# Two-layer decoder trunk: the sums of the third and fourth conditioning vectors of layer 0 shared out anew between VectorE, ScalarE and GpSimd

## What is computed

```python
c_act = silu(c)                                   # c: (1, 1024)
for l in range(2):
    mod = c_act @ w_ada[l] + b_ada[l]             # six vectors of 1024
    sh1, sc1, gt1, sh2, sc2, gt2 = split(mod, 6)
    h = x * (1 + sc1) + sh1
    y = hybrid_mixer(h, ...)                      # window attention + top-k attention picked by index scores
    x = layer_norm(alpha * x + (1 + gt1) * y, ...)
    h = x * (1 + sc2) + sh2
    y = swiglu(h, ...)
    x = layer_norm(alpha * x + (1 + gt2) * y, ...)
```

## Time and profile before

| | us |
|---|---|
| median of 3 runs (1275.62 to 1276.37) | 1276.03 |
| the profiled execution | 1276.25 |
| its span in the trace | 1274.6 |
| TensorE busy in it | 1235.8 (97%) |
| VectorE busy | 801.5 (63%) |
| ScalarE busy | 510.5 (40%) |
| GpSimd busy | 274.2 (22%) |

### The profile page before, as it was taken

One profiled execution on the slowest core, in us unless ns is written; L12 is line 12 of the kernel. 1 busy time (PEld: TensorE's weight loads), 2 busy tenths in 40 slices (PEclk: granted clock), 3 DMA queues, 4 the chain that ended last, 5 costly groups with the idle time before them and its releaser, 6 DMA issues. The chain is left out here.

```text
span 1274.6 us, 18347 instructions
## 1 busy us (share of the span) xinstructions
PE 1235.8 (97%) x6394; PEld 1031.6 (81%) x6394; DVE 801.5 (63%) x1400; ACT 510.5 (40%) x1027; POOL 274.2 (22%) x281
## 2 busy tenths in 40 slices
PE   6999989999999999999999999999999999999997
PEld 5778876889888888888888688778988888888886
DVE  6889997677777764333676699856733355433338
ACT  3555568345232212222145466862643321222220
POOL 4027236600111010000007367570000000000000
PEclk9999999999999999999999999999999999999999
DMA  9672012334878554222523120112232223332211
GB/s 358 240 270 79 33 51 67 132 116 150 279 264 270 193 168 175 90 93 98 171 94 117 66 67 2 37 63 84 75 124 99 97 101 132 99 98 89 94 65 66
DMA packets 44850, 158.30 MB, mean 124 GB/s; under 512 B 5872, under 2 KB 5872, under 8 KB 44784
## 3 DMA queue, kind: packets, MB, share of 16 engines
q1 hardware_dynamic: 30528, 109.07, 24.8%
q0 software_dynamic: 12960, 47.19, 10.9%
q10 hardware_dynamic: 1296, 1.17, 0.3%
HBM read 155.31 MB, written 2.10 MB: 123 GB/s over the span
## 5 line engine op out<-in xcount | busy, mean ns | idle before, releaser
L631 PE MATMUL bank<-hT_hi,w_hi 128*128 128x512 f32 x640 | 249.5, 390 | 0.0
L633 PE MATMUL bank<-hT_hi,w_lo 128*128 128x512 f32 x640 | 249.0, 389 | 0.0
L632 PE MATMUL bank<-hT_lo,w_hi 128*128 128x512 f32 x640 | 249.0, 389 | 0.0
L1967 DVE TENSOR_TENSOR w_lo<-w_raw,w_hi 128x1024 fp32r<-128x1024 f32 x88 | 107.9, 1226 | 147.0 <-ACT w_hi L1434 147.0
L1280 ACT ACTIVATE w_hi<-w_raw 128x1024 fp32r<-128x1024 f32 x96 | 100.7, 1062 | 202.8 <-PE bank L633 189.0
L1434 ACT ACTIVATE w_hi<-w_raw 128x1024 fp32r<-128x1024 f32 x88 | 93.0, 1057 | 161.1 <-PE bank L633 155.8
L631 PE MATMUL bank<-w_hi,hT_hi 128*128 128x512 f32 (+2 forms) x392 | 148.1, 378 | 2.9 <-ACT pq L1316 2.0
L1544 DVE TENSOR_TENSOR w_lo<-w_raw,w_hi 128x1024 fp32r<-128x1024 f32 x88 | 114.1, 1310 | 53.6 <-ACT w_hi L1280 52.2
L633 PE MATMUL bank<-w_hi,hT_lo 128*128 128x512 f32 (+2 forms) x392 | 142.6, 364 | 0.0
L632 PE MATMUL bank<-w_lo,hT_hi 128*128 128x512 f32 (+2 forms) x392 | 142.3, 363 | 0.0
L633 PEld LDWEIGHTS bank<-hT_hi,w_lo 128*128 128x128 f32 x640 | 120.1, 188 | 25.3
(11 more groups left out here) (207 smaller groups left out, 2199.5 us busy)
## 6 DMA issues: line engine op xcount, KB each, us to landing
w_raw<-in_weights SPq DMA_DIRECT2D x184, 512.0 KB, 3.5
ada_w<-in_w_ada POOLq DMA_DIRECT2D x80, 512.0 KB, 5.2
ada_w<-in_w_ada SPq DMA_DIRECT2D x4, 512.0 KB, 6.6
qT<-in_w_ada SPq DMA_DIRECT2D x4, 512.0 KB, 10.0
xs<-in_x SPq DMA_DIRECT2D x4, 512.0 KB, 15.4
g_row<-in_ln_row POOLq DMA_DIRECT2D x4, 512.0 KB, 5.2
b_row<-in_ln_row POOLq DMA_DIRECT2D x4, 512.0 KB, 6.1
trunk_out<-xs SPq DMA_DIRECT2D x8, 256.0 KB, 2.1
```

The lines of the kernel that those rows point to most:

```text
L631: pe.matmul(dst, a_hi, b_hi, start=first, stop=False)
L632: pe.matmul(dst, a_hi, b_lo, start=False, stop=False)
L633: return pe.matmul(dst, a_lo, b_hi, start=False, stop=last)
L1967: nc.vector.tensor_tensor(w_lo[:, s, :], w_raw[:, s, :], w_hi[:, s, :].bitcast(F32), ALU.subtract).then_inc(lo_ready, 1)
```

## The change

The last four pieces of group 2 (`ASIDE`, n = 20 to 23) leave VectorE. ScalarE scales each with one activation (`scale_aside`) into a buffer of its own: `g_row`, `b_row` and two halves of `pq[:, 1]`, which are free at that time; two of them stand before the evacuation of chunk 1, two behind it. GpSimd adds the four up with three additions of 128x1024 in `g_row`, between its issues of loads, and `reduce_mod(2)` sums both `ada_acc` and `g_row` on TensorE, with 16 products instead of 8. The slots of pieces 20 to 23 are loaded again when ScalarE has scaled them (`aside_scaled`), and counts of `ada_used` leave them out (`ada_count`). VectorE now sums all eight pieces of group 3 before the index scores: two before the `rope` calls on the index keys, six after `convert` of weight pieces 10 and 11. The four pieces amid the attention are gone, and GpSimd issues the loads up to piece 35 before its `rope` of the queries. `evacuate(0, 2, t)` waits for the three additions, and GpSimd's `ln_rows(1)` for `reduce_mod(2)`.

```diff
...
 QB_AT = (9, 21, 30, 45)
 
 
-ASIDE_AT = (12, 18, 24, 30)
-ASIDE_FROM = 3 * KD + 4
+ASIDE = range(2 * KD + 4, 3 * KD)
 
 WO_AT = (42, 47, 52, 57)
 GATE_AT = 63
...
             pT = sb("pT", [P, PT_RING, 512], on=att)
 
         prob = pq[:, 1]
+
+        aside = [g_row[:], b_row[:]]
+        aside += [pq[:, 1, 2 * n:2 * n + 2, :].rearrange("p a s -> p (a s)") for n in range(2)]
 
         y = pk[:].rearrange("p t n -> p (t n)").rearrange("p (b n) -> p b n", b=2)
 
...
 
             b, at = (2 + k // 4, (k % 4) * P) if g == 0 else (6, k * 64)
             return bank[b][:, at:at + n]
+
+        def ada_count(n):
+
+            return n if n <= ASIDE[0] else n - len(ASIDE)
 
         def columns_to(g):
 
...
             def ada_fetch(upto):
                 while fetched[0] < upto:
                     n = fetched[0]
-                    pool.wait_ge(ada_used, n - RING + 1)
+                    if n - RING in ASIDE:
+                        pool.wait_ge(aside_scaled, n - RING - ASIDE[0] + 1)
+                    else:
+                        pool.wait_ge(ada_used, ada_count(n - RING + 1))
                     if n < 2 * KD + RING:
 
                         pool.wait_ge(mod_reduced, 2)
...
                     ada_fetch(2 * KD + 4 + RING)
                     pool.wait_ge(tables_ready, 1)
                 if l == 0:
-                    ada_fetch(3 * KD + 4)
+                    ada_fetch(3 * KD + 2)
+                    for i in range(1, 4):
+                        pool.wait_ge(aside_scaled, i + 1)
+                        if i > 1:
+                            pool.wait_ge(aside_summed, i - 1)
+                        nc.gpsimd.tensor_tensor(aside[0], aside[0], aside[i], ALU.add).then_inc(aside_summed, 1)
+                        ada_fetch(3 * KD + (2, 4, 4)[i - 1])
+                    pool.wait_ge(aside_summed, 3)
                 else:
                     for t in range(T):
                         rope(l, 0, t)
...
                 if l == 0:
                     pool.wait_ge(small_in, 16 * 4)
                 if l == 0:
-                    ada_fetch(ASIDE_FROM + RING)
+                    ada_fetch(4 * KD + RING)
                 for t in range(T):
                     rope(l, 2, t)
                 for t in range(T):
                     rope_keys(l, t)
                 for i in range(64 + LAG_ROOT):
-                    if i in ASIDE_AT and l == 0:
-                        ada_fetch(ASIDE_FROM + RING + ASIDE_AT.index(i) + 1)
                     if i in ROPE_AT:
                         rope(l, 4, ROPE_AT.index(i))
                     if i == ROPE_AT[-1]:
...
                         gained_low_half(l, WO_AT.index(i))
                 if l == 0:
                     ada_fetch(5 * KD + RING)
+                    pool.wait_ge(mod_reduced, 3)
                 ln_rows(2 * l + 1)
                 for t in range(T):
                     rsqrt(l, 8 + t)
...
 
             def reduce_mod(g, b):
 
-                pe.wait_ge(ada_used, (g + 1) * KD)
+                pe.wait_ge(ada_used, ada_count((g + 1) * KD))
+                if g == 2:
+                    pe.wait_ge(aside_summed, 3)
                 for k in range(KD):
                     m = pe.matmul(bank[b][:, k:k + 1], ada_acc[:, g % 2, k * P:(k + 1) * P], ones[:, 0:1],
-                                  start=True, stop=True)
+                                  start=True, stop=g != 2)
+                    if g == 2:
+                        m = pe.matmul(bank[b][:, k:k + 1], aside[0][:, k * P:(k + 1) * P], ones[:, 0:1],
+                                      start=False, stop=True)
                 m.then_inc(mod_reduced, 1)
 
             def first_mod(g, vector, first):
...
                 src = bank[QB_BANK if c == 4 else BANKS[c] + t]
                 if c in (0, 2, 4):
 
+                    if l == 0 and c == 2:
+                        act.wait_ge(aside_summed, 3)
                     if l > 0 and c == 0:
                         act.wait_ge(qk_transposed, at_chunk(l - 1, 4, t))
                     elif l > 0 and c == 2:
...
                     nc.scalar.activation(v_a[:, t, 0:P], src[:, P:2 * P], ACT.Copy)
                     nc.scalar.activation(v_a[:, t, P:P + HD], src[:, P:P + HD], ACT.Copy).then_inc(proj_evac, 1)
 
+            def scale_aside(i):
+
+                n = ASIDE[i]
+                act.wait_ge(ada_in[n % RING], 16 * ((n - 2 * KD) // RING + 1))
+                if i < 2:
+                    act.wait_ge(mod_reduced, 2)
+                else:
+                    act.wait_ge(tables_ready, 1)
+                nc.scalar.activation(aside[i], ada_w[:, n % RING, :], ACT.Copy, scale=cc[:, 1, n % KD:n % KD + 1])\
+                    .then_inc(aside_scaled, 1)
+
             def copy_q(l, c, t):
                 act.wait_ge(qk_transposed, at_chunk(l, c, t))
                 if c == 4 and t == 0:
...
                 for c in range(2):
                     if c == 1:
                         convert(l, C0P[2] + 2)
+                    if c == 1 and l == 0:
+                        scale_aside(0)
+                        scale_aside(1)
                     for t in range(T):
                         if (l, c) != (0, 0):
                             evacuate(l, c, t)
                         if c == 0 and t == 1:
                             convert(l, C0P[1] + 2)
+                    if c == 1 and l == 0:
+                        scale_aside(2)
+                        scale_aside(3)
                     convert(l, C0P[c + 1] + 3 + c)
                 for t in range(T):
                     copy_q(l, 0, t)
...
                         residual(l, WO0, WO0_ORDER[0], True)
                         if l == 0:
                             ada_group(4, 4, 7)
-                    if i in ASIDE_AT and l == 0:
-                        n = ASIDE_FROM + ASIDE_AT.index(i)
-                        ada_group(n // KD, n % KD, n % KD + 1)
                 conv[0] += 4
 
             def feed(l, g):
...
                     convert(l, C0P[1] + 3)
                     ada_group(2, 2, 4)
                     convert(l, C0P[1] + 4)
-                    ada_group(2, 4, 6)
                     convert(l, C0P[2] + 1)
-                    ada_group(2, 6, 8)
                 convert(l, C0P[2] + 2)
+                if l == 0:
+                    ada_group(3, 0, 2)
                 for t in range(T):
                     rope(l, 1, t)
                 convert(l, C0P[3])
                 if l == 0:
-                    ada_group(3, 0, 4)
+                    ada_group(3, 2, 8)
                 for n in range(6):
                     for h in range(4):
                         add_index_head(l, n // 2, 4 * (n % 2) + h)
```

More of the change, by code:

```diff
@@ L267, in build_trunk @@
         ada_scaled = sem("ada_scaled")
+        aside_scaled = sem("aside_scaled")
+        aside_summed = sem("aside_summed")
         ada_summed = sem("ada_summed")
@@ L607, in _ @@
                         for j in range(KD):
-                            pool.wait_ge(ada_used, i * KD + (base + j - RING + 1))
+                            pool.wait_ge(ada_used, i * KD + ada_count(base + j - RING + 1))
                             pool.dma_start(ada_w[:, j % RING, :], w_ada[i + (base + j) // KD, (base + j) % KD])\
@@ L1121, in reduce_ada @@
                 def reduce_ada(i):
-                    pe.wait_ge(ada_used, i * KD + 5 * KD)
+                    pe.wait_ge(ada_used, i * KD + ada_count(5 * KD))
                     for k in range(KD):
@@ L1551, in ada_group @@
                     if k > 0:
-                        dve.wait_ge(ada_used, n)
+                        dve.wait_ge(ada_used, ada_count(n))
                     ada_piece(n, k, g)
@@ L1977, in ada_pieces @@
                         else:
-                            dve.wait_ge(ada_used, i * KD + n)
+                            dve.wait_ge(ada_used, i * KD + ada_count(n))
                             m = nc.vector.scalar_tensor_tensor(out=acc, in0=ada_w[:, n % RING, :],
```

## The result

The changed kernel takes 1285.51 us (median of 4, 1285.38 to 1285.56) against 1275.82 in the same series: 9.7 us longer, ratio 1.0076 with a 95% interval from 1.0061 to 1.0091. The prediction was 1279.8 with a range up to 1282.4: the sign was right, the size was not. The profiled execution took 1285.47, its span is 1283.8.

What follows compares the result with a forecast made beforehand. TensorE, 97% busy, was taken to bound the kernel. Front +6.2, sum +1.8 and attention -4.2 gave +3.8 us on the profiled 1276.25, so 1280.05; with the median 0.22 lower, 1279.8, range 1273.2 to 1282.4.

Steps and rivals of the forecast that it cites:

- Before, 24 was issued at 67.98 and took 5.7 us: Front, ahead of the ropes: loads 24 and 25 take 5.7 us again and land at 74.0 and 75.1.
- I take the middle, 4.3: Front: loads 30 and 31 take 4.3 us, between 3.7 and 4.8, and end at 95.35 and 96.65.
- How long they take no row shows: Front: said no profile row gives the duration of loads 30 and 31, so 4.3 us was assumed.
- an operation of VectorE with two inputs in SBUF and one of GpSimd do not overlap: Front: each waits for the other to finish, so GpSimd's additions, 2.35 us each, hold up VectorE's pieces and ropes.
- the walk built on it: Front, followed step by step: first rope at about 80.95 instead of 73.45, index sums at 96.65, 7.6 us late.
- I take 1.4 us as swallowed: Index scores: of VectorE's 7.6 us lateness 1.4 (0.7 to 1.7) does not reach TensorE, stopped +6.2 us.
- the row's own price for the same 8 blocks: TensorE's sum of group 2: 16 blocks for 8 cost +1.8 us, 1.6 to 2.0 at the ends.
- The attention, taken from layer 1: Layer 0's attention without its four pieces: -4.2 us of their 5.65, since layer 1 runs the same heads without them.
- The rival in which VectorE alone sets its pace: Attention: all 5.65 us come back; with nothing lost in the front, 1272.2; chance 0.14.
- the loads are quick: Front rival: every load takes 3.7 us, TensorE is 3.5 us late, 1277.1; chance 0.16.
- The sum given for the fit, +0.3: Whole change: with the skill's fit, a piece landing 3.2 us after issue, about +0.3 us, 1276.3.
- the first rival's walk: Front with every load at 3.7 us: ropes at 74.35, piece 31 at about 94.0, index sums 4.9 us late.

Runs made afterwards that it cites:

- e3: The changed kernel without GpSimd's three additions, all other work kept, the 16 blocks too: 1281.86 us, +5.5 against the kernel before.
- e1: The kernel before with only VectorE's order changed: all eight pieces of group 3 ahead of the index scores, nothing given away: 1277.11 us, +0.7.
- e4: The changed kernel with a fourth GpSimd addition folding in VectorE's half, so TensorE sums 8 blocks, not 16: 1282.25 us, +5.9 against the kernel before.
- e7: The changed kernel with the ropes of the index keys ahead of pieces 24 and 25 on VectorE: 1283.96 us, +8.4 against the kernel before.
- e5: The changed kernel with the 16 blocks cut in three by two dense products of chunk 4: 1283.63 us, +8.0 against the kernel before.
- e9: The kernel before with all of group 3 ahead of the index scores and TensorE's dense work in layer 0 one step ahead: 1273.57 us, -2.2.
- e2: The changed kernel with group 3 as before; pieces 20 to 23 still go to ScalarE and GpSimd, 16 blocks: 1279.96 us, +3.6 against the kernel before.
- e8: The changed kernel with ropes first, loads to 35 ahead of GpSimd's later additions, memsets early, a fourth addition, 8 blocks: 1275.47 us, -0.3 against the kernel before.
- b1: The kernel before with TensorE's sum of group 2 in 16 blocks, each taken a second time into unread columns: 1278.45 us, +2.8.
- e10: e8 with TensorE's dense work in layer 0 one step ahead as well: 1274.42 us, -1.4 against the kernel before.

## Why the prediction was wrong

- *"Before, 24 was issued at 67.98 and took 5.7 us"* was the first step that failed. Load 24 of the changed kernel was issued at 68.76 and took 7.7 us, load 25 took 8.1, and beside them are two weight pieces, at 7.1 us; the DMA engines are 0.89 busy from 66 to 72. That VectorE's three conversions now follow each other at once, so that SyncE asks for the two together, is the likely reason, which no run shows by itself. I had noted the fullness and kept the old figure. The first rope came 1.1 us later than forecast. In the same way "I take the middle, 4.3" for loads 30 and 31: 5.3 and 5.5, with loads 32 and 33 issued at 93.82 and 95.14 while they were under way and the engines at 1.00 from 94 to 98. All told the index sums came 2.4 us later than forecast (99.1 with the start taken out, against 96.65). I had counted the loads up to 35 as free on GpSimd's queue and not on the DMA engines. "How long they take no row shows" was true of the rows chosen and not of the trace before: load 25 took 6.1 us there, 26 and 27 took 6.2 and 6.9, and of the four loads between 82 and 86 the 4.8 of the earlier trace rows is the quickest. The issues at 83.19 and 84.51 before, and at 91.18 in the changed kernel:

```profile
ada_w<-in_w_ada POOLq DMA_DIRECT2D x1, 512.0 KB, 6.1
ada_w<-in_w_ada POOLq DMA_DIRECT2D x1, 512.0 KB, 6.0
...
ada_w<-in_w_ada POOLq DMA_DIRECT2D x1, 512.0 KB, 5.3
```

- *"an operation of VectorE with two inputs in SBUF and one of GpSimd do not overlap"* was right, and the walk built on it came out at 81 for the first rope (82.1 with the start taken out). The additions cost 2.5 us of lateness (e3). Two inputs seem not to be needed for it: the multiplication of piece 24 reads one piece and took 1.72 us instead of 0.75 beside the second addition (75.21 to 77.62).
- *"I take 1.4 us as swallowed"* failed: 0.2 in the change, 0.3 in e1, and less than nothing in e3, e4 and e7. In e1, at the full clock, the second group of heads ends 2.7 us late with sums 3.8 late, so 1.0 is swallowed there (96.40 against 94.41, its start 0.75 earlier); but the fourth group lasts 2.31 us instead of 1.60, and 0.7 is lost again. In the change the second group ran at 1.2 GHz and ended 9.8 late at once (104.42); at e1's pace it would have been some 0.8 less, an estimate, and the later groups waited no more. This, at 1.2 us, and the 2.4 of the loads and the ropes are 3.6 of the 5.2 us that were missing.
- *"the row's own price for the same 8 blocks"*, 1.8, was exact. What no step had was the lower clock behind 16 such blocks, 1.4 us in the profiled execution; with 8 blocks (e4) or blocks apart (e5) it was not there. The last 0.2 are the attention's.
- The attention, taken from layer 1, gave 4.0 for 4.2. The rival in which VectorE alone sets its pace fell: 5.65 us less on VectorE gave 4.0.
- The rival "the loads are quick" stood on the rows at 3.7 us; the four loads for which VectorE waits took 7.7, 8.1, 5.3 and 5.5, and the quickest of the stretch 4.1 (26 and 28). The Trainium skill's fit for such a load ("DMA: Bandwidth & Descriptors", "Anatomy of one DMA"), 3.2, is further off still; the traces do not agree with it here. The sum given for the fit, +0.3, is also not what the walk makes of it: loads 0.5 us shorter move the first rival's walk by 0.5, from +1.1 to +0.6.
- The signs asked for were seen: piece 24 waited for (7.8 us where 5 were forecast), 25 stretched, index sums past 92, ropes past 76, and the attention scores at 141.7 where 136.4 was forecast.

## What to carry to other kernels

When work moves to an engine that shares the SBUF with the one relieved, count it on both: here GpSimd's additions held VectorE for longer than the freed pieces had taken. When loads move to an earlier stretch, price them by how full the DMA engines will be with everything that moved there. And before giving work away, look whether the stop of the bounding engine can be filled by its own next dense step: with VectorE's sums reordered and nothing given away, that made the largest gain over the kernel before (e9); the reordering without it was a draw (e1). And a duration that a sum rests on is to be looked up for all its like nearby: the trace before had loads of 6.0 us where the forecast took 4.3.

## What was not expected of the hardware

- The granted clock fell to 0.50 in or just behind 32 one-column products that kept TensorE busy all the time (the change, e2), and held in the profiled executions in which dense products stood between them (e5) or there were half as many (e4, e8). It is no fixed rule: it held behind 32 in b1's profiled execution, and fell behind 16 and a wait of 0.37 us in e10's. The Trainium skill ("Trainium Kernel Development and Optimization", "Performance Expectations") calls matmul busy time a bad measure of how close a kernel is to what the chip can do, because matmuls are pipelined. The rows give one more reason to mistrust it: PE's busy time is 4.00 of 4.00 us at a clock of 1.00 and at 0.57 alike, and only the column of the clock tells them apart.
- An operation of VectorE was held from before GpSimd's addition began: piece 25 starts at 78.21 and ends at 82.32, GpSimd's third addition runs only from 78.83 to 81.23, and from 77.57 to 78.83 GpSimd issues two loads. The same was seen in e2, where a rope starts at 77.83. Issues alone do not hold VectorE: in the kernel before, pieces are added in 1.28 us beside them. Which part of GpSimd's sequence takes the hold so early was not tried. The Trainium skill ("SBUF — State Buffer", "SBUF: two separate sides") describes a pair of ports that VectorE, with two inputs in SBUF, and GpSimd share as an exclusive lock, held for a whole instruction by whichever starts first. That one of them blocks the other entirely agrees with the rows (0.42 us become 2.64 and 3.41 beside an addition of 2.4); that the first to start goes through does not, by the starts that the profile shows for piece 25 and that addition. The profile's spans on GpSimd are rough, so this does not settle it.
